# The second tile's convolution moved from POOL to VectorE, its halves around the first pair of dots

## The reference

```python
def ssd_mixer(z, xbc, dt, conv_w, conv_b, ...):
    # causal depthwise convolution, CONV_WIDTH = 4 taps, over 1024 channels
    xbc = conv(xbc, conv_w, padding=[(3, 0)]) + conv_b
    xbc = silu(xbc)
    ...                       # chunked scan with xs, bm, cm cut from xbc

def peer(h, wq, k1, k2, u, v):
    q = (xt @ wq).reshape(ntok, 8, 2, 128)
    s1, s2 = q[:, :, 0] @ k1.T, q[:, :, 1] @ k2.T
    ...                       # top 16 of each, top 16 of their 256 sums: eidx, gate
    act = gelu(einsum('td,tkd->tk', xb, u[ib])) * gate
    return einsum('tk,tkd->td', act, v[ib])       # 8 heads x 16 experts per token

h   = layer_norm(ALPHA * x + mix)
out = layer_norm(ALPHA * h + peer(h))
```

## Time and profile before

| | us |
|---|---|
| median of 3 runs | 835.3 (829.94, 835.3, 835.62) |
| the profiled execution, its own time | 832.65 |
| its span, first to last instruction | 830.9 |
| busy: TensorE matmul / VectorE / ScalarE / POOL | 568.8 / 542.3 / 449.3 / 297.9 |
| software queue of the gathers, share of the 16 DMA engines | 78.6% |
| bytes read from HBM | 299.49 MB |

### The profile page before, as it was taken

The page is one execution under the profiler, slowest core; times in us unless marked ns, Lnnn a source line. Parts: engine busy times, 40 slices in busy tenths (PEclk is TensorE's granted clock), DMA queues, the critical chain, the costliest instruction groups (busy, mean ns, idle before and its releaser), DMA issues.

```text
span 830.9 us, 10111 instructions
## 1 busy us (share of the span) xinstructions
PE 568.8 (68%) x3343; PEld 473.9 (57%) x3343; DVE 542.3 (65%) x1364; ACT 449.3 (54%) x805; POOL 297.9 (36%) x279
## 2 busy tenths in 40 slices
PE   7989999887879888864545555525566565454596
PEld 4458577575569887853544445524455564454542
DVE  3487574485777574848585858469857576767454
ACT  1025137455667665756565657527766566565532
POOL 0000005642444334453535353414754435344400
PEclk9989999899979899967878776767776767867789
DMA  8991005899999999999999999999999999999992
GB/s 300 386 355 52 1 1 204 297 397 354 341 416 411 410 410 410 419 421 422 422 420 422 420 420 420 422 421 382 411 421 421 421 423 422 422 421 423 422 422 109
DMA packets 58521, 301.08 MB, mean 362 GB/s; under 512 B 5576, under 2 KB 16112, under 8 KB 25712
## 3 DMA queue, kind: packets, MB, share of 16 engines
q0 software_dynamic: 36864, 268.45, 78.6%
q1 hardware_dynamic: 20400, 31.92, 10.8%
q10 hardware_dynamic: 1216, 0.19, 0.1%
HBM read 299.49 MB, written 1.05 MB: 362 GB/s over the span
## 4 chain that ended last, share of the span: by engine, by line
DMA 40%; PE 26%; DVE 19%; issue 6%; ACT 6%; POOL 2%; another core or an unknown queue 1%; DVEq 0%; SPq 0%; POOLq 0%; ACTq 0%
DMA arena<-in_expert_uv,expert 34%; PE bank L652 6%; PE bank L502 5%; DMA arena<-in_peer_wq 5%; PE bank L633 5%; DVE arena L1482 5%; PE bank L672 3%; ACT arena L1010 3%; PE bank L514 2%; POOL arena L455 1%; ACT weight L1000 1%; PE bank L617 1%; DVE score L1459 1%; DVE score L1461 1%
## 5 line engine op out<-in xcount | busy, mean ns | idle before, releaser
L455 POOL DMA_INDIRECT arena<-in_expert_uv,expert x256 | 281.4, 1099 | 489.5 <-PE bank L652 260.0
L652 PE MATMUL bank<-ident,arena 128*128 128x128 f32 x1920 | 302.7, 328 | 218.5 <-ACT arena L1010 211.8
L1482 DVE SCALAR_TENSOR_TENSOR arena<-x_sb,arena 128x1024 f32<-128x1024 f32 x256 | 307.9, 1229 | 172.0 <-DMA arena<-in_expert_uv,expert 168.5
L652 PEld LDWEIGHTS bank<-ident,arena 128*128 128x128 f32 x1920 | 279.9, 173 | 241.9 <-ACT arena L1010 233.2
L1010 ACT ACTIVATE arena<-arena,weight 128x1024 f32<-128x1024 f32 x240 | 257.1, 1138 | 2.2
L995 ACT ACTIVATE gelu<-dots 128x4 f32<-128x4 f32 (+2 forms) x76 | 15.5, 204 | 216.7 <-DVE arena L1482 209.1
L502 PE MATMUL bank<-arena,x_t 128*128 128x512 f32 (+1 forms) x128 | 55.1, 585 | 6.1 <-DMA arena<-in_w_idx 6.1
L633 PE MATMUL bank<-x_t,arena 128*128 128x128 f32 x384 | 50.9, 297 | 11.6 <-DMA arena<-in_peer_wq 11.6
L1000 ACT ACTIVATE weight<-gelu,gate 128x1 f32<-128x1 f32 x256 | 55.9, 284 | 3.5
L633 PEld LDWEIGHTS bank<-x_t,arena 128*128 128x128 f32 x384 | 49.7, 213 | 12.2 <-DMA arena<-in_peer_wq 12.2
L502 PEld LDWEIGHTS bank<-arena,x_t 128*128 128x128 f32 x128 | 25.3, 206 | 30.3 <-issue 26.4
(11 more groups left out here) (200 smaller groups left out, 487.6 us busy)
## 6 DMA issues: line engine op xcount, KB each, us to landing
arena<-in_w_in SPq DMA_DIRECT2D x5, 2048.0 KB, 19.8
arena<-in_peer_wq SPq DMA_DIRECT2D x6, 1024.0 KB, 7.4
arena<-in_w_out SPq DMA_DIRECT2D x2, 2048.0 KB, 18.2
arena<-in_expert_uv,expert POOLq DMA_INDIRECT x256
mix<-in_peer_wq SPq DMA_DIRECT2D x2, 1024.0 KB, 16.1
arena<-in_w_idx SPq DMA_DIRECT2D x4, 304.0 KB, 6.7
x_t<-in_x_columns SPq DMA_DIRECT2D x4, 256.0 KB, 5.8
x_sb<-in_w_in SPq DMA_DIRECT2D x1, 1024.0 KB, 9.5
```

The costliest lines, as they stand in the source:

```text
L455: pool.indirect_dma_start(out=arena[:, slot * SLOT:(slot + 1) * SLOT], out_offset=None, in_=expert_uv, in_offset=bass.IndirectOffsetOnAxis ...
L652: last = mm(banks[2 * tile + k // 4][:, (k % 4) * P:(k % 4 + 1) * P], lhsT=arena[:, at + k * P:at + (k + 1) * P], rhs=ident[:, :], is_tran ...
L1482: ins = stt(rows, x_rows[:, bass.ds(tile * D_MODEL, D_MODEL)], 1.0, rows, ALU.mult, ALU.mult, accum_out=dots[:, parity, j:j + 1])
```

## The change

`convolve_late` and its placement go, with the scratch `tap_product` and the semaphore `late_tap`. VectorE calls `convolve(1, 0)` ahead of the first pair of dots of unit 0 and `convolve(1, 1)` behind it. The gather into slot 1 now waits for `conv_ready` at 4, both halves of both tiles.

```diff
-        tap_product = view(arena, at + 1536, 4, P)
...
-        consts_t_ready, late_tap = sem("consts_t_ready"), sem("late_tap")
+        consts_t_ready = sem("consts_t_ready")
...
                             pool.wait_ge(slot_used, len(before) - before[::-1].index(slot))
-                        elif slot in last_readers:
+                        elif slot == 1:
+
+                            pool.wait_ge(conv_ready, 2 * TILES)
+                        else:
                             wait_job(pool, last_readers[slot])
...
                     ).then_inc(rows_in[slot], 16)
-                    if isinstance(u, int) and u == 0 and j in LATE_TAPS:
-                        for n, k in LATE_TAPS[j]:
-                            convolve_late(n, k)
-
-            LATE_TAPS = {1: ((0, 0), (0, 1)), 3: ((0, 2), (1, 0)), 5: ((1, 1),), 7: ((1, 2),)}
-
-            def convolve_late(n, k):
...
             finish_gate(0, 0)
+            convolve(1, 0)
             dot_slots(0, 0, 0, 0)
+            convolve(1, 1)
             dot_slots(0, 0, 0, 1)
```

## The result

The changed kernel takes 825.56 us (median of 20 runs, 824.48 to 830.48), the kernel before 834.4 (median of 20, 827.61 to 836.59). The ratio is 0.9915, with a 95% interval of 0.9895 to 0.9934: faster by about 0.85%, 7 us. The medians alone differ by 8.8 us, the means by 7.4. The profile of the changed kernel was taken in an execution of 830.48 us, the longest of its twenty, so it shows the steps of the change well and the gain badly; a second profile stands with the first experiment.

A forecast was written before the change was run, and what follows sets the result against it. Full transfer queues bound the second half, so only starting them earlier or filling empty queue time helps. Second pair 2.7, transposes 1.6 and key-score copy 0.4 sum to 4.7 us: 835.3 to 830.6, forecast 830.5, range 825.5 to 837.5.

The forecast's parts named there:

- The outer cases: The rivals' times, 826.8 (More than the chain shows) and 836.8 us (Slower), widened by about 1.5 us for the range.
- the forecast's own bounds: Smallest and largest gain on the chain, 1.7 and 5.8 us, giving 829.5 to 833.6 us; chance 0.57.
- POOL's time ahead of the gathers: Twelve instructions leave POOL: j=2 goes at about 137.8 for 139.87, j=4 at 144.9 for 149.28, j=9 about 5 us earlier.
- VectorE's taps: Two halves add 7.0 us; half 0 hides in the 6.91 us wait for j=0, half 1 runs behind the first dots.
- The second pair: Dots of gathers j=2 and j=3: the last ends at 148.7 against 151.43, 2.7 us earlier (bounds 1.7 and 3.2).
- the gather at 139.87: Gathers lose time to dots: this one took 1.66 us under the first dot, against 0.94 at 133.77; put at nothing.
- The clock: TensorE's idle time before the second pair's transposes falls from 3.31 to 0.6 us; transposes take 2.1 for 3.67, gaining 1.6.
- The copy of the key scores: ScalarE's copy at 157.98 comes near 153.3, after 2.7 + 1.6 + 0.4 = 4.7 us won on the chain.
- Absorbed: Rival: a later wait that doesn't move with the earlier gathers takes the time back; gain 0 to 1 us, 835; chance 0.20.
- More than the chain shows: Rival: the new order keeps queues full through the 132 to 168 us stretch; 8.5 us, 826.8; chance 0.13.
- from 835.3 the same 4.7 us give 830.6: Carries the profiled execution's gain (832.65 to 828.0) over to the median of three runs; forecast 830.5.
- Slower: Rival: VectorE's taps hold the memory port, so j=0 goes 2.9 us later and TensorE's clock falls; 836.8; chance 0.10.

The follow-up runs named there:

- the first experiment: The run e1_again: the changed kernel measured once more, no edit, for a second profile; median 825.88 us, ratio 0.99.
- f5_busy_j1: Changed kernel, with four idle-work POOL instructions on scratch added behind gather j=1 only; 828.17 us, ratio 0.9943.
- e2_half0: Kernel before, with only half 0 convolved on VectorE; half 1 stays on POOL, one tap each behind gathers j=3, j=5, j=7; 826.3 us, ratio 0.9903.
- e3_pool_busy: Changed kernel, with POOL's twelve instructions back at their old places, writing scratch that nobody reads; 833.3 us, ratio 1.0011.
- e4_no_taps: Changed kernel, with the second tile's three earlier taps left out of the computation; 825.61 us, ratio 0.9908.
- e1_again: Changed kernel once more, no edit, for a second profile; median 825.88 us, ratio 0.99.
- f2_load_late: Changed kernel, with the load of head 2's query weights issued some 3 us later, behind six used slots; 838.15 us, ratio 1.0052.
- f6_busy_j3: Changed kernel, with four idle-work POOL instructions on scratch added behind gather j=3 only; 829.67 us, ratio 0.9957.
- i2_after_load_first: Changed kernel, with gather j=9 held back until head 2's weights have landed; 825.5 us, ratio 0.9878.
- b1_before: Kernel before, no edit, run again for a second profile; one execution of 830.66 us, median 833.37 beside it.

## Why the prediction was right, and where its size was off

The sign was right, and so was most of the mechanism. The forecast was 4.7 us; the medians moved by 8.8 and the ratio says 7. The range held by luck: the median of 825.56 lies 0.06 us inside its lower end of 825.5, and well below the 829.5 to 833.6 that the forecast's own bounds give. (The outer cases of 826.8 and 836.8, widened by 1.5 us, give 825.3 to 838.3, not 825.5 to 837.5; it makes no difference here.)

*POOL's time ahead of the gathers.* Right. j=2 was forecast 5.4 us behind the first gather and went at 5.6, j=4 at 12.5 and went at 12.5, j=9 at about 28 and went at 28.7. f5_busy_j1 loses 2.3 us by POOL's time ahead of j=2 and j=3 alone, and e2_half0 keeps the whole gain with half the taps moved. e3_pool_busy undoes the gain, but there POOL holds VectorE up as well.

*VectorE's taps.* Right, 3.48 us for a half against 3.49. Half 0 costs nothing and half 1 some 0.2 us at most, as e4_no_taps shows.

*The second pair.* 2.7 us were forecast, with bounds of 1.7 and 3.2. The two profiles of the changed kernel have 2.1 and 3.0 (fourth dot's end 17.0 and 16.1 us behind the first gather, 19.1 before). The forecast gives gather j=3 some 1.3 us (139.1 to 140.4); it began beside a dot and took 1.66 and 1.89 us, a loss that the prediction reads off the gather at 139.87 but puts nowhere in its sum.

*The clock.* Right: 0.93 us of idle time in place of 3.31, transposes at 2.13 us. The copy of the key scores was forecast 4.7 us earlier and came 4.0 us earlier in the first profile, and 4.9 us earlier in the second.

*Absorbed* (the rival) happened in the first profile: 4.0 us won at the key scores are 1.1 at the end (the spans are 830.9 and 828.7, and from the first gather on 698.5 and 697.4). Its place is the one wait that doesn't move with TensorE, the landing of a weight load that shares the engines with the gathers. I had written that I found nothing in the chain that isn't released by something that shifts too. The load's issue shifts; its time to land is its own, within six us in e1_again and 21.5 us in the first profile.

*More than the chain shows* is nearest to the median, but not for the reason that it gives (queues kept full). The term that was missing is the same load in the kernel before. The step that was mis-sized is "from 835.3 the same 4.7 us give 830.6": the sum was made in a profile of 832.65 in which that load was in time, and then taken from a median whose executions mostly have more in them. With the load halved the two kernels lie 3.0 us apart (828.05 and 825.06), and the kernel before alone falls by 6.4. That is measured. That in its executions of 835 to 839 TensorE waits for head 2's weights is argued from it, from f2_load_late and from the late packets in both profiles of that kernel, and not shown, since neither is such an execution. Part of its spread may come from the clock too: idle times of 2.42, 2.74 and 3.31 us ahead of the second pair in three profiles lie on both sides of the fall.

*Slower* (the taps hold back the first gathers) fell: the gathers of 131.26 and 132.69 took 1.12 and 0.98 us beside half 0, against 1.09 and 0.94 before.

*Still open:* why, if it is so, the load is late so much more often in the kernel before. In both it is issued with the same event as gather j=9, and asked for some 19 us later (165.4 to 184.06 before, 160.0 to 179.44 in e1_again). The change moves gather j=8 away from it, from 5.0 us ahead of the load to 9.0 (e1_again). That alone doesn't explain it: in e2_half0 j=8 goes 4.0 us ahead of the load (156.34 and 160.32), and all its six executions lie under 827.6. Nor is it traced why the stretch from the end of the v projection to the wait for head 4's weights is 108.5 us in the first profile of the kernel before and 106.7 in the second (165.36 to 273.84, 165.42 to 272.13).

## What to carry to other kernels

Read the spread of the runs beside the profile before summing: where a kernel's executions lie 11 us apart, one profile shows one of its kinds, and a change may take away the other kind as well. When a chain is moved forward, look for the waits on it that have a duration of their own, a transfer that shares its engines above all, compare the time to their landing with the time to their first use, and do so in more than one execution. And when work is put on an engine only to take its time, check that it doesn't slow a neighbour.

## What the runs showed of the hardware

- A half of taps on VectorE, twelve instructions with both inputs in SBUF, took 3.48 us alone and beside gathers, and 6.26 to 7.71 us beside POOL's two-input instructions on SBUF (four halves in e3_pool_busy, f5_busy_j1 and f6_busy_j3). In 3.7 us beside them three taps ran, in 3.2 us ahead of them ten (e3_pool_busy). By the Trainium skill, SBUF — State Buffer, "Who interferes with whom", the shared port is an exclusive lock that one engine holds for its whole instruction; the trace agrees, and the price is on both: POOL's add took 2.05 us in f6_busy_j3 where its neighbour took 1.19.
- A gather that began while a dot ran took 1.66 to 2.00 us in the two profiles of the changed kernel, in place of 0.94; beside the short taps it took 0.94 to 1.13.
- TensorE ran its 16 transposes of the second pair at full speed behind idle times of 2.11 and 2.42 us (2.13 and 2.14 us), and slower behind 2.70, 2.74 and 3.31 us (3.00, 3.67 and 3.67 us). The idle time alone doesn't decide: further on, at about 176 us, the same transposes behind the same 2.22 us took 2.13 us in f2_load_late (clock 1.00) and 3.58 in e1_again (clock 0.50).
- The load of 1 MB from SP's queue landed in 5.4 to 5.5 us in i2_after_load_first, f5_busy_j1 and f6_busy_j3, in 15.2 us in b1_before and 21.5 us in the changed kernel's first profile, where all but some 50 packets were in after six us, and in 26.8 us when it was issued behind three gathers (f2_load_late).
- POOL issued a load of 128 x 2048 words from a strided source in 0.95 us, no longer than a gather.
